# Larger buffers and longer DMA runs in the expert loop, sums kept in PSUM, and attention scores on half of the array's rows

## What is computed

```python
logits = einsum('bnqkgd,bnskd->bnkgqs', qr, kc) * scale + bias        # attention scores, heads of 64
h = x + mixed @ w_out
u = rms_norm(h, norm_ffn_g)
top_vals, top_idx = lax.top_k(u @ w_router + b_router, 4)
top_w = softmax(top_vals)
# for each expert e, on the tokens routed to it:
hh = u[tok] @ w1[e] + b1[e]                                           # 1024 -> 2048, even columns gate, odd ones linear
hb = swiglu_clamped(hh)                                               # 1024
acc[tok] += (hb @ w2[e] + b2[e]) * wt                                 # 1024 -> 1024
out = rms_norm(h + acc, norm_final_g)
```

## Time and profile before

| | us |
|---|---|
| median of 3 runs | 1490.92 (1490.73 to 1491.5) |
| the profiled execution | 1489.51 |
| its span, first to last instruction | 1487.7 |
| TensorE busy | 1388.5 (93%) |
| VectorE busy | 503.7 (34%) |
| ScalarE busy | 321.5 (22%) |
| GpSimd busy | 22.8 (2%) |
| DMA | 464.26 MB, mean 312 GB/s |

### The profile page before, as it was taken

How to read it: one execution, slowest core, us unless ns; L and a number is a source line. 1 busy time by engine, 2 the same in 40 slices (tenths; PEclk the granted TensorE clock), 3 DMA queues, 4 the chain that set the end, 5 groups by cost and what they waited for, 6 DMA issues and landing times.

```text
span 1487.7 us, 19865 instructions
## 1 busy us (share of the span) xinstructions
PE 1388.5 (93%) x7262; PEld 674.6 (45%) x7262; DVE 503.7 (34%) x1075; ACT 321.5 (22%) x642; POOL 22.8 (2%) x33
## 2 busy tenths in 40 slices
PE   6999999999999699999999999999999999999997
PEld 3888787555886333333333333333333333333332
DVE  1055466677223432223322332223222322232223
ACT  3124333344100121211111111212121212111121
POOL 3000000000000000000000000000000000000000
PEclk9999999999999799999999999999999999999999
DMA  9923243141945699999999999999999999999993
GB/s 237 248 85 108 91 142 113 57 113 60 307 150 191 210 388 410 410 409 410 409 410 409 410 410 410 410 410 410 409 410 409 410 410 410 410 409 410 409 410 151
DMA packets 164807, 464.26 MB, mean 312 GB/s; under 512 B 24199, under 2 KB 59247, under 8 KB 164741
## 3 DMA queue, kind: packets, MB, share of 16 engines
q1 hardware_dynamic: 162544, 457.27, 81.1%
q0 software_dynamic: 1872, 6.13, 1.4%
q10 hardware_dynamic: 356, 0.41, 0.1%
HBM read 462.42 MB, written 1.10 MB: 312 GB/s over the span
## 4 chain that ended last, share of the span: by engine, by line
PE 84%; DVE 4%; DMA 4%; ACT 3%; SPq 3%; issue 1%; POOL 0%; POOLq 0%; ACTq 0%; DVEq 0%
PE bank L1168 81%; DMA ring<-in_w 4%; SPq L401 3%; DVE arena L1106 1%; ACT arena L760 1%; DVE arena L1114 1%; ACT arena L757 1%; PE bank L1534 1%; DMA arena<-in_meta 0%; PE bank L1192 0%; PE bank L1526 0%; PE bank L1253 0%; PE bank L1428 0%; PE bank L1255 0%; ACT arena L560 0%
## 5 line engine op out<-in xcount | busy, mean ns | idle before, releaser
L1168 PE MATMUL bank<-ring,arena 128*64 128x512 f32 (+3 forms) x2808 | 675.3, 593 | 52.9 <-ACT arena L760 45.6
L1168 PEld LDWEIGHTS bank<-ring,arena 128*64 128x64 f32 (+2 forms) x2808 | 219.8, 141 | 432.2 <-issue 373.8
L1168 PE MATMUL bank<-arena 128*128 128x64 bf16 (+6 forms) x2773 | 370.0, 337 | 13.6 <-DVE arena L1072 4.1
L1168 PE MATMUL bank<-arena,ring 128*128 128x256 f32 (+1 forms) x1184 | 270.5, 387 | 2.6 <-ACT decays L598 1.0
L1168 PEld LDWEIGHTS bank<-arena 128*128 128x128 bf16 (+3 forms) x2773 | 172.4, 124 | 221.0 <-issue 145.9
L1168 PEld LDWEIGHTS bank<-arena,ring 128*128 128x128 f32 x1184 | 223.8, 191 | 39.4 <-issue 1.4
L1102 DVE TENSOR_TENSOR arena<-arena,bank 128x512 f32<-128x512 f32 x128 | 88.1, 688 | 291.8 <-PE bank L1168 291.8
L1106 DVE TENSOR_TENSOR arena<-bank,cols 128x512 f32<-128x512 f32 x32 | 22.1, 692 | 290.2 <-PE bank L1168 290.2
L754 ACT ACTIVATE arena<-bank 128x256 f32<-128x256 f32 x32 | 12.3, 385 | 359.7 <-PE bank L1526 359.7
L757 ACT ACTIVATE arena<-arena 128x256 f32<-128x256 f32 x64 | 26.7, 417 | 172.2 <-DVE arena L1114 172.2
L764 ACT ACTIVATE arena<-bank 128x512 f32<-128x512 f32 x64 | 34.7, 594 | 125.1 <-PE bank L1168 125.1
(11 more groups left out here) (221 smaller groups left out, 588.0 us busy)
## 6 DMA issues: line engine op xcount, KB each, us to landing
ring<-in_w SPq DMA_DIRECT2D x320, 1024.0 KB, 18.1
arena<-in_w SPq DMA_DIRECT2D x64, 1024.0 KB, 18.1
ring<-in_w_in SPq DMA_DIRECT2D x30, 1024.0 KB, 5.4
ring<-in_w_ssm SPq DMA_DIRECT2D x8, 1024.0 KB, 6.0
ring<-in_w_in SPq DMA_DIRECT2D x16, 256.0 KB, 7.1
ring<-in_w_att SPq DMA_DIRECT2D x16, 256.0 KB, 6.7
ring<-in_w_out SPq DMA_DIRECT2D x4, 1024.0 KB, 4.8
arena<-bias_rows POOLq DMA_DIRECT2D x1, 2048.0 KB, 12.5
```

The costliest lines, as they stand in the source:

```text
L1168: return tn.matmul(o, lhsT, rhs, start=first, stop=last, skip_group_check=True)
```

## The change

1. **Loads.** `w1` in four pieces and `w2` in two (`PARTS` = 6), each 2 MB with one run of 16 KB per partition: a partition holds two neighbouring rows of `w1` or four of `w2`. Six buffers (`even_bufs`) and four more for `w1` of odd experts (`odd_bufs`).
2. **First matrix.** So that a partition's four rows of `w2` meet the right hidden units, the columns of `w1` are read in groups of four with a step of eight (`p (k h m c r)`), one group for each half of the array's columns. The two halves of `w1` are no longer separate stretches: each piece serves both. The bias rows are read likewise, and the hidden transposes take every second column (`hsw[:, half, q::2]`). The row order of `w1` also changes the order of the input features: `un`, the norm gain and the router matrix are laid out to match.
3. **Sums in PSUM.** `residual` puts `acc` into banks 0 to 3 by a product with the identity; every scatter accumulates there. VectorE's four adds per expert go. `w2`'s results for the two column halves lie in the two halves of one bank, so the scatter has 64 rows and one copy serves (`ysb`, L764).
4. **Order.** The gather of the next expert, the scatter and the weight transposes follow the whole first matrix and precede the hidden transposes. VectorE makes the selection matrices two experts ahead.
5. **Start of the loop.** First loads: two pieces behind `y_done`, one behind `T_END`, three behind `branch_used` and `m_done`, three behind `h_ready`, one behind `lg_ready`. GpSimd's clearing of `ysb` and the load of `b2` wait for `up_done`; ScalarE's square waits for `b1_spread`.
6. **Scores.** Keys in `kT`, two heads on 64 partitions each; each matmul uses 64 rows, and the two heads alternate.
7. **End.** ScalarE squares the four banks one by one, VectorE multiplies out of the banks in four instructions. `gfin` is loaded by SyncE behind the last expert loads.

```diff
+PARTS = 6
+BUF = 2 * SLOT
...
-        kz = at(R + 2048, KV, NT)
+        kT = at(R + 2048, KV // 2, NT)
...
+        even_bufs = [at(6400, BUF), ring_pair(4), at(R, BUF), at(R + 6144, BUF), ring_pair(1), ring_pair(5)]
+        odd_bufs = [ring_pair(0), ring_pair(2), ring_pair(3), at(0, BUF)]
...
-        w1_v = w1.rearrange("e (s k p) (h c) -> e h s p k c", p=P, k=2, h=2)
-        w2_v = w2.rearrange("e (h c b p) n -> e h b p c n", p=P, h=2, c=2)
+        w1_v = w1.rearrange("e (s p k) c -> e s p (k c)", p=P, k=2)
+        w2_v = w2.rearrange("e (h p r) n -> e h p (r n)", p=P, r=4)
...
             def first_experts():
...
+                sp.wait_ge(branch_used, 12)
+                fetch(3, sources[0][3], 0)
+                fetch(4, sources[0][4], 0)
+                sp.wait_ge(m_done, 8)
+                fetch(5, sources[0][5], 0)
+                sp.wait_ge(h_ready, 2)
+                for i in range(3):
                     fetch(i, sources[1][i], 1)
+                sp.wait_ge(lg_ready, 1)
+                fetch(3, sources[1][3], 1)
...
+                    pool.wait_ge(up_done, 1)
                     pool.memset(ysb, 0.0).then_inc(b2_cleared, 1)
...
+            for i in range(4):
+                act.wait_ge(last_sc_ready, i + 1)
+                squared(sc.activation(glu.rearrange("p a b -> p (a b)"), bank[i][:, :], ACT.Square,
+                                      accum_out=ssq[:, i:i + 1]), 13 + i + 1)
...
-                done(v.tensor_scalar(un[:, c, :], acc[:, c, :], rstd[:, c:c + 1], None, ALU.mult), un_ready, 4 + c)
+                done(v.tensor_scalar(un[:, c, :].rearrange("p (s k q) -> p s q k", s=4, k=2),
+                                     acc[:, c, :].rearrange("p (s q k) -> p s q k", s=4, k=2),
+                                     rstd[:, c:c + 1], None, ALU.mult), un_ready, 4 + c)
                 ch.link(v.tensor_copy(upart[:, 0, c, :], un[:, c, :]))
+                dve.wait_ge(resid_done, c + 1)
...
-            def scatter_add(s):
-
-                for i in range(4):
-                    c, n = divmod(i, 2)
-                    dve.wait_ge(sc_ready, s * 4 + (i + 1))
-                    a = acc[:, c, 512 * n:512 * n + 512]
-                    done(v.tensor_tensor(a, a, bank[6 + n][:, :], ALU.add), sc_added, s * 4 + (i + 2))
...
-                for half in range(2):
-                    b, kk = bank[half], kz[:, 2 * (t // 4) + half, :]
-                    mm(b[:, 0:NT], qT[:, t, 0:BLK], kk[:, 0:NT], True, True)
-                    ins = mm(b[:, NT:LK], qT[:, t, BLK:SEQ], kk[:, 0:META + BLK], True, True)
+
+                for queries, k1, c0 in ((slice(0, BLK), NT, 0), (slice(BLK, SEQ), META + BLK, NT)):
+                    for half in range(2):
+                        r = slice(HD * half, HD * half + HD)
+                        ins = mm(bank[half][:, c0:c0 + k1], qT[r, t, queries], kT[r, t // 4, 0:k1], True, True)
...
+            def residual(c):
+
+                pe.wait_ge(h_done, 2 * c + 2)
+                for n in range(2):
+                    ins = mm(bank[2 * c + n][:, :], ident, acc[:, c, 512 * n:512 * n + 512], True, True)
+                ins.then_inc(resid_done, 1)
+
...
+            def scatter(n):
+
+                pe.wait_ge(ye_saved, n + 1)
+                pe.wait_ge(s2_saved, n + 1)
+                for c in range(2):
+                    for half in range(2):
+                        r = slice(CAP * half, CAP * half + CAP)
+                        ins = mm(bank[2 * c + half][:, :], s2[r, P * c:P * c + P], ysb[r, :], False, True)
+                return ins
+
+            def expert(t, b, pair, odd):
...
+                pe.wait_ge(usel_ready, t + b + 1)
+                for i in range(4):
+                    expert_arrived(pe, i, t, pair, odd)
+                    w = expert_buf(i, odd)[0].rearrange("p (k h m c r) -> p k h m c r", k=2, h=2, c=2, r=4)
+                    for half in range(2):
                         for kk in range(2):
+                            k = 2 * i + kk
                             for c in range(2):
+                                ins = mm(bank[4 + half][64 * c:64 * c + 64, :], usel[:, k, :], w[:, kk, half, :, c, :],
+                                         False, k == KT - 1)
+                        if i == 3 and half == 0:
+                            ins.then_inc(hid_ready, 1)
+                    ins.then_inc(slot_used, 1)
+                gather_wait = t * 1 + b * 2 + 1
+                gather(gather_wait)
+                scatter(t)
+                weight_transposes(t + b + 1)
                 for half in range(2):
                     pe.wait_ge(hs_ready, t * 2 + half + 1)
                     for q in range(2):
-                        ins = tn.transpose(bank[5][:, P * q:P * q + P], hsw[:, half, P * q:P * q + P], ident)
+                        ins = tn.transpose(bank[4 + half][:, P * q:P * q + P], hsw[:, half, q::2], ident)
                     ins.then_inc(hT_ready, 1)
```

More of the change, by code:

```diff
@@ L200, in hybrid_layer @@
[L200 to L207 removed]
+        b1raw = at(R + 10240, 2 * FF)
+        b1all = at(10496, 2 * FF, dt=BF16)
+        b1mid, b1lo = at(R + 4096, 2 * FF, dt=BF16), at(R + 5120, 2 * FF, dt=BF16)
@@ L442, in single @@
             def single(sources, odd, used):
-                for i in range(DOUBLED.stop, SLOTS):
+                for i in range(DOUBLED.stop, PARTS):
                     sp.wait_ge(slot_used, used + (i + 1))
@@ new lines, in usel_save @@
+            def usel_save(n):
+                dve.wait_ge(gat_ready, n + 1)
+                v.tensor_tensor(usel, bank[7][:, :].rearrange("p (k s) -> p k s", k=KT),
+                                col_gffn.unsqueeze(2).to_broadcast([P, KT, CAP]), ALU.mult).then_inc(usel_ready, 1)
+            def expert(t, e, b):
+                for half in range(2):
+                    if half == 0:
+                        dve.wait_ge(hid_ready, t + 1)
+                    else:
+                        dve.wait_ge(slot_used, t * PARTS + 4)
+                    hv = bank[4 + half][:, :].rearrange("p (f two) -> p f two", two=2)
@@ L1173, in _ @@
             tn.transpose(bank[4][:, 0:120], rows[0:120, 0, :], ident[0:120, 0:120])
-            tn.transpose(bank[4][:, 128:160], rows[0:32, 1, :], ident[0:32, 0:32]).then_inc(rows_T, 1)
+            tn.transpose(bank[4][:, 128:152], rows[0:24, 1, :], ident[0:24, 0:24])
+            for k in range(2):
+                ins = tn.transpose(bank[4][:, 160 + 4 * k:164 + 4 * k], gffn4[0:4, k::2], ident[0:4, 0:4])
+            ins.then_inc(rows_T, 1)
             pe.wait_ge(tab_ready, 1)
@@ L1470, in _ @@
                         router(0)
+                        residual(0)
+            residual(1)
             ffn_transposes(1)
@@ L1501, in expert, with weight_transposes @@
                         for c in range(2):
-                            ins = mm(bank[4][:, CAP * k:CAP * k + CAP], upart[:, part, c, P * k:P * k + P],
+                            ins = mm(bank[7][:, CAP * k:CAP * k + CAP], upart[:, part, c, P * k:P * k + P],
                                      gsel[:, c, :], part == 0 and c == 0, part == 2 and c == 1)
                 ins.then_inc(gat_ready, 1)
+            def weight_transposes(n):
+                pe.wait_ge(gw_ready, n + 1)
+                for c in range(2):
+                    ins = tn.transpose(bank[6][:, P * c:P * c + P], gwt[:, c, :], ident)
+                ins.then_inc(s2_ready, 1)
@@ L1505, in expert @@
                 for half in range(2):
                     for c in range(2):
-                        c0 = 1024 * half + 512 * c
-                        mm(bank[half][64 * c:64 * c + 64, :], bsel[0:3 * E, :], b1all[0:3 * E, c0:c0 + 512], True, False)
-                pe.wait_ge(usel_ready, t + 1)
-                for half in range(2):
-                    for s_ in range(4):
-                        i = 4 * half + s_
-                        expert_arrived(pe, i, t, pair, odd)
-                        w, _ = expert_slot(i, odd)
+                        mm(bank[4 + half][64 * c:64 * c + 64, :], bsel[0:3 * E, :], bv[0:3 * E, half, :, c, :], True, False)
@@ L1520, in expert @@
-                        ins.then_inc(slot_used, 1)
-                    if half == 0:
-                        pe.wait_ge(ye_saved, t * 2 + 2)
-                        scatter(t)
-                        for c in range(2):
-                            ins = tn.transpose(bank[5][:, P * c:P * c + P], gwt[:, c, :], ident)
-                        ins.then_inc(s2_ready, 1)
-                pe.wait_ge(s2_saved, t + 1)
+                                ins = mm(bank[4 + half][64 * c:64 * c + 64, :], usel[:, k, :], w[:, kk, half, :, c, :],
+                                         False, k == KT - 1)
@@ L1547, in _ @@
-            pe.wait_ge(b2_in, 16)
+                    expert_arrived(pe, 4 + half, t, pair, odd)
+                    w = expert_buf(4 + half, odd)[0].rearrange("p (c q n) -> p c q n", c=2, q=2)
+                    for c in range(2):
```

(5 more changed lines are left out.)

342 lines of the change are left out of this document (157 added, 185 removed).

## The result

The changed kernel takes **1439.21 us** (median of 4 runs, 1439.1 to 1439.7) where the kernel before, on the same chip, takes 1490.83 (1489.52 to 1491.5): a ratio of 0.9655, 95% interval 0.9639 to 0.9672, or 51.6 us less. The forecast was 1441. The profiled execution took 1439.1 with a span of 1437.3; the sum had said 1438.0. So close a hit calls for suspicion: it shows the sum, not its terms.

The account below looks back on a forecast made before the run. Two bounds 2% apart, TensorE and the DMA stream, then the stream alone: first buffer 515.2, start 3, stream 904.5, scatter at 1427.9, tail 10.1, span 1438.0, plus 1.8 and 1.4: 1441 us, range 1422 to 1472.

Parts of the forecast that it names:

- What bounds the kernel: Expert stretch before: two bounds 2% apart, TensorE with waits 30.05 us an expert, DMA stream 30.7; only lowering both helps.
- TensorE's work: One expert's TensorE time in the changed kernel: 27.1 to 29.0 us, depending on the scatter, against 30.05.
- The strided operand: First matrix read in groups of four float32 with a step of eight: no cost taken, 14 us more if slow.
- The stream: Expert loads in 16 KB runs: 422 GB/s instead of 410, bounds 410 and 430, so 29.8 us an expert.
- The front: Way to the first expert: terms sum to -0.6 us, matmuls start at 511.8, first buffer free at 515.2.
- Start of the stream: Start-up cost of the expert weight stream: 3 us taken instead of 5.8.
- The end: After the last byte at 1422.7: semaphore 1 us, half a second matrix 3.5, copy 0.7, scatter at 1427.9.
- The tail: From the last scatter to the end of the span: about 10.1 us, where it took 12.3 before.
- Longer runs bring nothing: Rival on the expert loads: the stream stays at 410 GB/s, 26.5 us more, 1468 us; chance 0.15.
- TensorE stays the bound: Rival on the experts: slow scatter and array shape changes, about 29.5 us each, 1470 us (1450 to 1485); chance 0.10.
- The strided operand is slow: Rival on the first matrix: 14 us more, an expert takes 42, 1870 us, slower; chance 0.07.
- Stream at 430: Rival on the expert loads: the stream goes at 430 GB/s, 1424 us, or 1431 if TensorE holds it; chance 0.06.

Follow-up runs that it names:

- the stream alone: Kernel before with its 1 MB expert loads in one run of 8 KB per partition, weights wrongly ordered: 1486.57 us, ratio 0.9975.
- the rest alone: Changed kernel with expert loads in four runs of 4 KB per partition instead of one of 16 KB: 1478.55 us, ratio 0.9921.
- The two order experiments: Changed kernel, `w2` asked for ahead of the next `w1`: from expert 26 on, 1431.94 us; from expert 25 with a step at 24, 1428.35 us.
- e7_gather_twice: Changed kernel with the 48 gather products of each expert done twice, nothing added to the stream: 1444.45 us, ratio 0.9691.
- e2_runs4: Changed kernel with expert loads in four 4 KB runs per partition, still 2 MB to a transfer, weights wrongly ordered: 1478.55 us, ratio 0.9921.

## Why the prediction was right, and where it wasn't

**What bounds the kernel.** Right, and tested from both sides: 4 us for the stream alone, 12 for the rest alone, 52 for both.

**TensorE's work.** The forecast of 27.1 to 29.0 us was too dear; the chain has 26.0. The first matrix takes 10.50 us for three of its four pieces, 14.0 in all, and the second 7.1 for both halves (1418.90). Mis-sized was the scatter: 1.99 us of TensorE where 2.15 was the favourable bound and the middle was taken. Row halves do run side by side. Even at that bound the sum gives 27.1, though. Much of the last microsecond is that it adds durations of groups which overlap at their ends: the second matrix lasts 7.1 us, forecast 7.3, and the group behind it starts after 6.9 (555.62 and 562.53). The 0.2 us and more that changes of array shape might cost don't show up. TensorE has 29.3 - 26.0 = 3.3 us to spare in each expert.

**The strided operand.** Right: 10.50 against 10.47 us.

**The stream.** The mechanism was right, the size was off: 429 GB/s, not 422. The step that failed is the continuation of the series. From the bursts it took 0.7 and 0.35 ns per KB for the two doublings, 2.8% in all. Measured from 410 over 422 to 429 they are 1.12 and 0.63 ns per KB, 4.4%. The bursts moved 4 KB runs at 425 GB/s, the long stream at 410; differences taken from the bursts were too small for the stream. 429 is within the bound of 430. The Trainium skill (DMA: Bandwidth & Descriptors, Bandwidth) gives 425 GB/s for 16 MB from HBM under a ceiling of 435; this trace, at 429, stands between. Worth: 904.5 - 889.7 = 14.8 us sooner.

**The front.** Forecast -0.6 for the first expert: 511.8, its first buffer free at 515.2. Measured: about 514.7. Inside, two terms were off. The scores gave 4 us up to the first block sum (473.99 before), not 2.0, by more than the upper bound. The residual product of 1.96 us (forecast 1.7) lies on the path, and at the second block sum only 490.35 - 488.39 = 2.0 are left. The permuted write takes 1.13 us where 0.75 stood: +0.4, forecast 0.5. At the gather 508.81 - 506.10 = 2.7 are gained, 2.1 more than the 0.6 forecast. Of these 2.1, 1.6 are lost again before the first buffer is free, 0.5 ahead of its forecast: the weight transposes (0.67 us) now stand between the gather and the bias rows, and the first matrix starts while the granted clock is still low (0.58 from 510 to 512, 1.00 from 512), where before it started at 512.42. Which of them took how much wasn't separated. The forecast of the front was right within 0.5 us, with terms that were not.

**Start of the stream.** 3 us forecast. By the same reckoning 514.7 + 889.7 + 4.1 (the gap) = 1408.5, and the last byte comes at 1412.5: 4.0, of which 1.2 are `gfin`, which the sum hadn't counted.

**The end.** This step failed. The prediction had one half of the second matrix behind the last byte, 1 + 3.5 + 0.7 = 5.2 us; it is 14.2. It took for granted that a stream-bound stretch ends stream-bound, and did not follow the last six loads through `last_two`. That the queue doesn't run dry, as its text on the buffers says, is true of the middle (429 GB/s throughout) and false here. The chain leaves the loads at 1365.37, 61.3 us ahead of the scatter, and from there TensorE is the bound. What the prediction noted as gained at the end, 12.8 us of expert work down to 4.2, wasn't gained at all: 13.7 us before, 14.2 after. The jump in the order adds the gap of 4.1. The two order experiments show both parts.

**The tail.** 1437.3 - 1426.68 = 10.6 us, forecast 10.1. Outside the span 1439.21 - 1437.3 = 1.9 us are left, forecast 3.2: the 1.4 by which the median of before lay above its profiled execution was chance and didn't come again. So of the 2 us between forecast and median, 1.3 are this.

**The sum as it came out.** 1438.0 - 0.5 (first buffer) - 14.8 (rate) + 4.1 (gap) + 1.0 (start) + 9.0 (end) + 0.5 (tail) = 1437.3, the span. A rate that was better than forecast paid for an end that was worse: that the time was met so closely is luck. By the prediction's own signs it should have been wrong. It named a dropped clock inside the stretch and a queue that runs dry, and both came: the first was hidden by the stream but for its last fall, the second cost 4.1 us, and the rate outweighed them.

**The rivals.** Longer runs bring nothing: refuted by the three rates. TensorE stays the bound: refuted for the middle, true from 1365 on, though not for the rival's reasons (a slow scatter, changes of array shape) but by the order of the loads. The strided operand is slow: refuted. Stream at 430: this one came true in its rate, and its 1424 was missed by the end above all; with the order mended the kernel takes 1428.35.

## What to carry to other kernels

Where two resources stand within a few per cent of each other, time each change alone and both together before either is thrown away: 4 and 12 us alone were 52 together. Where a stream is the bound, follow the last loads one by one to the last instruction, in the order of asking and in the order of use; a change of order belongs some experts ahead of the end, in steps so small that the queue always has a free buffer next. And a sum that meets the measured time is no proof of its terms: look up each of them in the trace.

## What the runs showed of the hardware

**A cost per DMA run.** About 9 ns for each run on an engine beside 37.6 ns per KB, on one line from 4 to 16 KB (159.8, 310.6, 611.1 ns), independent of the size of the transfer at 4 KB.

**Row halves for float32.** Products of 64 rows on different halves and into different banks overlap almost fully: eight instructions of 512 columns in 1.99 us, where eight with 128 rows take 3.43 to 3.96, and the scores of a pair in 0.70 us less than their 1.4.

**The clock falls at some waits, and their length doesn't say at which.** In after it falls at about every second expert in the middle, when a second matrix has waited for its load. Windows of 2 us in after, at the second matrix of one expert:

```profile
1246.00:1248.00 2.00, 0.10 (x2) 0.10 (x4) 0.00 (x0) 0.14 (x1) 0.00 (x0) 1.00 1.04 442
1248.00:1250.00 2.00, 2.00 (x8) 0.62 (x10) 0.00 (x0) 0.00 (x0) 0.00 (x0) 0.74 0.98 418
1250.00:1252.00 2.00, 2.00 (x6) 0.49 (x4) 0.00 (x0) 0.00 (x0) 0.00 (x0) 0.50 1.00 426
1252.00:1254.00 2.00, 2.00 (x12) 0.76 (x10) 0.00 (x0) 0.00 (x0) 0.00 (x0) 0.91 1.00 426
```

A wait of 2.25 us ends at 1247.90, and the clock falls to 0.50, the level of 1.2 GHz; 16 matmuls take 5.38 us there instead of 3.68. Other experts have waits of 2.1 us and keep 1.00, and so does one with 2.26:

```profile
689.97 3.65 PE L1191 MATMUL bank<-ring,arena 128*64 128x512 f32 x16 [2.26 <-DMA ring<-in_w]
```

With waits up to 1.3 us (e7_gather_twice) no window of 10 us between 600 and 1390 is below 1.00. But e2_runs4 waits longer, 3.40 and 1.56 us at one expert, and its profiled execution doesn't lose the clock in the middle either. Its second matrix:

```profile
1004.88 3.65 PE L1190 MATMUL bank<-ring,arena 128*64 128x512 f32 x16 [3.40 <-DMA ring<-in_w]
```

and the window of e2_runs4:

```profile
600.00:900.00 300.00, 255.05 (x1612) 107.89 (x1610) 49.39 (x140) 36.49 (x70) 0.00 (x0) 1.00 1.03 410
```

Nor does the kernel decide it alone: of the four executions of e2_runs4 three have a mean granted clock of 0.990 or 0.991 and one has 0.963, at 1478.67 us, so the same kernel can lose it too; at which waits that execution lost it isn't recorded. What decides is open. It costs little here, since a slower second matrix is hidden by the stream; at 1365.37 it lies on the path and costs about 1.5 us.
